# Expert weights as separate gate and up chunks, and all gate matmuls ahead of all up matmuls

## The reference, cut to what matters

```python
def expert_block(args):
    tok, e = args
    xb = xt_pad[tok]
    gate, up = jnp.split(xb @ w_gu[e] + b_gu[e], 2, axis=-1)
    gate = jnp.minimum(gate, SWIGLU_LIMIT)
    up = jnp.clip(up, -SWIGLU_LIMIT, SWIGLU_LIMIT)
    act = (up + 1) * (gate * jax.nn.sigmoid(SWIGLU_ALPHA * gate))
    return act @ w_dn[e] + b_dn[e]
```

## Time and profile before

| | |
|---|---|
| runs | 2408.28, 2408.59, 2414.71 us (median 2408.59) |
| profiled execution: its own time | 2408.47 us |
| profiled execution: span of the trace | 2406.7 us |
| mean granted TensorE clock | 0.963 |
| PE busy | 2178.1 us (91% of the span) |
| DVE, ACT, POOL busy | 747.0, 482.2, 65.4 us |
| moved by DMA | 591.29 MB in 158854 packets |

### The profile page before, as it was taken

One profiled execution on the slowest core, in us unless ns is written; L12 is line 12 of the kernel. 1 busy time (PEld: TensorE's weight loads), 2 busy tenths in 40 slices (PEclk: granted clock), 3 DMA queues, 4 the chain that ended last, 5 costly groups with the idle time before them and its releaser, 6 DMA issues.

```text
span 2406.7 us, 29048 instructions
## 1 busy us (share of the span) xinstructions
PE 2178.1 (91%) x11393; PEld 1161.2 (48%) x11394; DVE 747.0 (31%) x1825; ACT 482.2 (20%) x934; POOL 65.4 (3%) x79
## 2 busy tenths in 40 slices
PE   5999996899999998999889986997989997999998
PEld 4744453333333333333333334644454446888873
DVE  1696232122222221222211213242022254787100
ACT  1011111111111111111111101032021105887100
POOL 0000000000000000000000001000000000212000
PEclk8999997999999999999999998999999997999999
DMA  9554664769999998999966996443233141132241
GB/s 346 201 175 165 225 231 189 326 265 418 418 418 417 418 418 331 418 418 418 418 245 273 418 394 244 144 154 126 105 118 140 70 154 65 71 106 71 82 173 43
DMA packets 158854, 591.29 MB, mean 246 GB/s; under 512 B 5323, under 2 KB 6927, under 8 KB 125887
## 3 DMA queue, kind: packets, MB, share of 16 engines
q1 hardware_dynamic: 152512, 573.08, 60.8%
q0 software_dynamic: 4384, 16.40, 1.9%
q10 hardware_dynamic: 1887, 0.81, 0.1%
HBM read 589.23 MB, written 1.05 MB: 245 GB/s over the span
## 4 chain that ended last, share of the span: by engine, by line
PE 81%; DMA 6%; ACT 4%; DVE 4%; issue 2%; DVEq 1%; ACTq 0%; SPq 0%
PE PS L591 24%; PE PS L861 17%; PE PS L579 10%; PE PS L883 9%; PE PS L1049 4%; DMA W<-in_w_gu 3%; PE PS L895 2%; DMA W<-in_w_dn 2%; PE PS L854 1%; PE PS L1119 1%; PE PS L818 1%; PE PS L648 1%; DVE BIG L1833 1%; PE PS L831 1%; DVE BIG L1829 1%
## 5 line engine op out<-in xcount | busy, mean ns | idle before, releaser
L591 PE MATMUL PS<-W,BIG 128*128 128x512 f32 x1344 | 586.3, 598 | 5.0 <-DVE BIG L2245 2.9
L861 PE MATMUL PS<-W,BIG 128*64 128x512 f32 x2048 | 451.1, 598 | 3.2 <-DMA W<-in_w_gu 3.2
L591 PEld LDWEIGHTS PS<-W,BIG 128*128 128x128 f32 x1344 | 256.9, 192 | 325.1 <-issue 318.3
L861 PEld LDWEIGHTS PS<-W,BIG 128*64 128x64 f32 x2048 | 148.5, 138 | 305.3 <-issue 293.7
L579 PE MATMUL PS<-BIG,W 128*128 128x256 f32 x1088 | 240.8, 384 | 2.1 <-ACT BIG L348 2.1
L883 PE MATMUL PS<-W,BIG 128*64 128x512 f32 x1024 | 226.8, 595 | 8.4 <-ACT BIG L1317 8.4
L579 PEld LDWEIGHTS PS<-BIG,W 128*128 128x128 f32 x1088 | 209.5, 193 | 33.2 <-ACT BIG L348 3.3
L1827 DVE TENSOR_SCALAR BIG<-PS 128x512 f32<-128x512 f32 (+1 forms) x38 | 24.7, 650 | 426.7 <-PE PS L861 380.4
L883 PEld LDWEIGHTS PS<-W,BIG 128*64 128x64 f32 x1024 | 70.6, 137 | 144.0 <-issue 126.8
L1313 ACT ACTIVATE BIG<-BIG 128x512 f32<-128x512 f32 x32 | 20.2, 630 | 492.3 <-DVE BIG L1827 492.3
L1049 PE MATMUL PS<-BIG,W 128*128 128x256 f32 x448 | 105.3, 389 | 0.0
(11 more groups left out here) (453 smaller groups left out, 1917.8 us busy)
## 6 DMA issues: line engine op xcount, KB each, us to landing
W<-in_w_gu SPq DMA_DIRECT2D x128, 2048.0 KB, 14.1
W<-in_w_dn SPq DMA_DIRECT2D x64, 2048.0 KB, 15.6
W<-in_w_in SPq DMA_DIRECT2D x24, 2048.0 KB, 8.9
W<-in_w_mod SPq DMA_DIRECT2D x12, 2048.0 KB, 9.7
W<-in_gla_w_in SPq DMA_DIRECT2D x10, 2048.0 KB, 7.8
W<-in_s_w_in SPq DMA_DIRECT2D x8, 2048.0 KB, 8.9
W<-in_s_w_glu SPq DMA_DIRECT2D x8, 2048.0 KB, 8.0
W<-in_w_out SPq DMA_DIRECT2D x6, 2048.0 KB, 8.0
```

The lines of the kernel that those rows point to most:

```text
L591: ins = pe.matmul(ps[:, t, :], lhs(i * KT + k)[:, t * P:(t + 1) * P], w[:, k, :], start=i + k == 0, stop=last_chunk and k == KT - 1)
L861: ins = pe.matmul(PS[hh[h], g, :], XET[:, k, :], gu_w(k)[:, g * D + h * CH:g * D + (h + 1) * CH], start=False, stop=k == KT - 1, skip_grou ...
```

## The change

The w_gu chunks are cut another way. Before, chunk j held the whole rows of two k slices (two pieces of 8 KB for each partition). Now chunks 0 and 1 hold the gate columns of k 0 to 3 and 4 to 7, and chunks 2 and 3 the up columns, so that each partition gets four pieces of 4 KB. The matmul loops are turned: g is outermost, in the main part and in the extra block. gate_done is counted half way through the 32 matmuls instead of after the 30th. chunk_done for chunk 1 is counted one matmul later, at the first up matmul, since the last gate matmul already counts gate_done; the other counts stay at the same place.

```diff
@@ SP @@
                             if j < 4:
-                                sp.dma_start(flat_w.rearrange("p (a n) -> p a n", a=2), gu[:, 2 * j:2 * j + 2, :]) \
+                                sp.dma_start(flat_w.rearrange("p (a n) -> p a n", a=4),
+                                             gu[:, 4 * (j % 2):4 * (j % 2) + 4, (j // 2) * D:(j // 2 + 1) * D]) \
                                     .then_inc(w_landed[j], 16)
@@
-        def gu_w(k):
-            return W[:, k // 2].rearrange("p k n -> p (k n)").rearrange("p (a n) -> p a n", a=2)[:, k % 2, :]
+        def gu_w(k, g):
+            return W[:, 2 * g + k // 4].rearrange("p k n -> p (k n)").rearrange("p (a n) -> p a n", a=4)[:, k % 4, :]
@@ extra_block @@
-                for k in range(KT):
-                    if k % 2 == 0:
-                        landed(e, k // 2)
-                    for g in range(2):
+                for g in range(2):
+                    for k in range(KT):
+                        if k % 4 == 0:
+                            landed(e, 2 * g + k // 4)
                         for q in range(4):
-                            ins = pe.matmul(PS[qq[q], g, 0:T], XETX[:, k, :], gu_w(k)[:, g * D + q * T:g * D + (q + 1) * T],
+                            ins = pe.matmul(PS[qq[q], g, 0:T], XETX[:, k, :], gu_w(k, g)[:, q * T:(q + 1) * T],
                                             start=False, stop=k == KT - 1, skip_group_check=True)
@@ expert @@
-                for k in range(KT):
-                    if k % 2 == 0:
-                        landed(e, k // 2)
-                    for g in range(2):
+                for g in range(2):
+                    for k in range(KT):
+                        if k % 4 == 0:
+                            landed(e, 2 * g + k // 4)
                         for h in range(2):
-                            ins = pe.matmul(PS[hh[h], g, :], XET[:, k, :], gu_w(k)[:, g * D + h * CH:g * D + (h + 1) * CH],
+                            ins = pe.matmul(PS[hh[h], g, :], XET[:, k, :], gu_w(k, g)[:, h * CH:(h + 1) * CH],
                                             start=False, stop=k == KT - 1, skip_group_check=True)
-                        if k == KT - 1 and g == 0:
+                            if k == 0 and g == 1 and h == 0:
+                                ins.then_inc(chunk_done, 1)
+                        if k == 3:
+                            ins.then_inc(chunk_done, 1)
+                        elif k == KT - 1 and g == 0:
                             ins.then_inc(ev("gate_done"), 1)
-                    if k % 2 == 1 and k < KT - 1:
-                        ins.then_inc(chunk_done, 1)
                 ins.then_inc(ev("up_done"), 1)
```

## The result

The changed kernel takes 2418.41 us in the median of 20 runs (2416.57 to 2427.64); the kernel before took 2409.46 in 20 runs (2405.66 to 2416.94). The ratio is 1.0038, with a 95% interval of 1.003 to 1.0047. The forecast was 2420.3, inside a range of 2413 to 2428. By the medians the change costs 9.0 us; by the two profiled executions, which are rather low for the kernel before and rather high for the one after, 11.25 us (2408.47 and 2419.72).

The account below looks back on a forecast made before the run. The DMA queue was taken to set the pace for 23 expert loads, PE to bound the rest. Longer w_gu chunks cost 12.4 us, the early gate gains 0.6, sum 11.8: 2408.5 + 11.8 = 2420.3 us, range 2413 to 2428.

Parts of the forecast that it names:

- What bounds the kernel: Experts' stage: the DMA queue sets the pace in series of 14 and 9 loads, so 23 loads lie on the path.
- The cut of the w_gu chunks: w_gu loads in the two series: 4 KB pieces make each of 92 chunks 0.135 us longer, 12.4 us (11.5 to 13.3).
- the first stall: PE's first wait for weights in a series: forecast at its 8th expert, expert 10, and expert 24 in the second.
- the 14.1 that I reckoned: Time the queue has in hand before PE stalls: 11 x 1.36 - 0.86 = 14.1 us.
- Half rows cost what whole rows do: w_gu pieces of half a row priced like w_dn's 4 KB pieces, 410 GB/s; rival of dear half rows, 2449 us, chance 0.06.
- The line of 8 ns and 37 ns per KB: Queue time per piece, drawn through the 8 and 4 KB rates; gives 84 ns for 2 KB, where w_in_2 has 84.7.
- Piece length is free: Rival for the weight loads: one rate whatever the piece, only extra blocks count, 2407.9 us, no change; chance 0.10.
- Early gate: Activation: gain 0 in an ordinary expert, 0.15 us in each of four extra blocks, 0.6 us in all.
- Turned loops: Main part: the same 32 matmuls with the same tiles in another order, no cost.
- chunk_done of chunk 1 one matmul later: Load issue: two passes, some 0.4 us later, hidden; without cover it would be 0.4 us once per series.
- the cover of 1.5 us: Start of a series: the second load is asked for 1.5 us before the queue is free, which hides the later count.
- The clock falls in the new stalls: Rival for PE after waits of 1.9 us: five at 1.4 us would add 7 us, 2427 us; chance 0.04.

Follow-up runs that it names:

- the queue relieved: Kernel before and changed kernel, each with the second w_dn chunk cut to 32 bytes per partition, for timing only: 2390.88 us and 2384.48 us.
- the paired rows: Kernel before with its loops, each partition holding pairs of neighbouring weight rows (w_gu 16 KB, w_dn 8 KB pieces): 2401.45 us, ratio 0.997.
- the filler: 12 more matmuls in each extra block's gap; on the turned extra block 2408.47 us, on the late-count kernel 2426.18, with paired rows and turned extra block 2396.85.
- the late gate: Changed kernel with gate_done counted near the end of the up matmuls again, in main part and extra block: 2423.61 us, ratio 1.0057.

## Why the prediction was right

**What bounds the kernel.** Right: 23 expert loads on the path, as two unbroken transfers. It is what made a change of packet sizes worth anything; with the queue relieved the same change gained 6.4 us.

**The cut of the w_gu chunks, 92 x 0.135 = 12.4 us.** Right in mechanism, too small in size. The period gives (30.72 - 30.10) / 4 = 0.155 us a chunk, 14.3 in all, and the two series together 15.5. The chunk now takes 5.12 us, the upper end of what I had for w_dn; I took the middle. Of the 1.2 us between 14.3 and 15.5 the slow second 5 us of each series hold 1.1. It goes with the first stall, which came one expert sooner than forecast: at 30.72 - 28.74 = 1.98 lost per expert, seven experts use up 13.9, and PE waited 0.75 in the seventh, so the series had 13.9 - 0.75 = 13.1 in hand and not the 14.1 that I reckoned.

**Half rows cost what whole rows do.** Right: 409 GB/s in w_gu and 410 in w_dn. Pieces of 2 KB of the same matrix came to 387, of 16 KB and 8 KB together to 426. The line of 8 ns and 37 ns per KB (of 1000 bytes) held from 2 to 16 KB: it gives 427 and 421 GB/s for the two pieces of the paired rows, and 426 was measured over both. The 17 us that I expected of them, where 7.5 came, rested on a slip in working it out, and it left out the late loads ahead of expert 0 and the half clock in extra blocks.

**Piece length is free** (rival): refuted. The Trainium skill, "DMA: Bandwidth & Descriptors", section "Specifications", has 512 B as enough for the full rate; in these runs 2, 4 and 8 KB differ by 9%. The estimate of 0.23 us per expert load, by the Trainium skill, the same page, section "Why small descriptors are slow (HBM only)", compares with a measured 0.62.

**Early gate.** Right where it was priced: 0 in an ordinary expert (the wait is 0.44 before and after), 0.15 us in an extra block (1.52 to 1.37). What it may do through the clock was not in the prediction. Over all ten profiles without the filler, 10 of 26 blocks that no weight load holds up ran partly at half clock with an early gate, and 10 of 18 with a late one. That doesn't tell them apart, and whether part of the 5 us of the late gate comes from there stays open.

**Turned loops: 0.** Right as far as it shows: ordinary experts kept 28.74, and turning the extra block alone cost nothing.

**chunk_done of chunk 1 one matmul later: hidden.** Probably wrong, by 0.55 us a series. The second load is asked for 0.83 us later and not 0.4, and the cover of 1.5 us left out that a load moves nothing in the first microsecond behind its issue (0 GB/s from 498.88 to 499.88). All seven profiles with this count have 4.26 or 4.27 us to the second load of the first series and 337 to 373 GB/s in the second 5 us; the six without it have 3.43 or 3.42 and 424 to 439. The shorter pieces came with it each time, so it was not tested by itself.

**The clock falls in the new stalls** (rival): no. After each stall of 1.47 us the next 16 passes took 3.65, full speed. In the extra block of expert 25 it did fall: behind a wait of 3.20 us, where the kernel before waited 1.38, 32 passes took 3.58 instead of 1.93. The queue's last landing comes later than that (1220.74), so nothing came of it. By luck one half clock even went away: the last down half of expert 16 took 1.93 instead of 3.30, which is the -1.35 in the table.

**What was missing.** The loads of a ring do not only serve their own stage. The first w_gu loads run ahead of the experts beside a small load that the path waits for, and shorter pieces gave 1 to 2 us back there, and some of the clock behind it. The forecast came out close (11.8 against 11.25 by the profiles, 9.0 by the medians) because this and the clock's luck offset a queue term that was 3.1 us too small (15.5 against 12.4). That closeness is luck; the mechanism is not.

## What to carry to other kernels

Where a stage runs its DMA queue without a pause, the length of a contiguous piece is a price on the path, even between 4 and 8 KB; where a turned loop would cut rows, price that first, and give each partition whole or neighbouring rows if you can. Price it from the kernel's own saturated stretches by piece length, and count only the loads between the first issue with an empty queue and the landing that PE waits for. A later request for the second load counts too when the queue starts empty. Where the queue has slack, the same cut is free or better, so the answer of one stage is not that of another.

## What the runs showed of the hardware

- The rate of a saturated queue of 2 MB loads by piece: 387 GB/s at 2 KB (also with loads of 1 MB), 410 at 4 KB, 421 at 8 KB, 426 with 16 KB for w_gu and 8 KB for w_dn.
- A load of 512 KB from POOL's queue lands later the longer the pieces of the stream beside it: it was waited for until 9.9 to 10.6 us behind its issue at 8 KB and 11.6 at 16 KB, and had landed after 8.4 to 8.8 us at 4 KB.
- Gaps of 1.4 to 1.5 us in the extra blocks leave TensorE's clock at 2.4 GHz in one execution and drop it to 1.2 in the next, 1.7 us each time. After a wait of 3.19 us the same code took 1.93 us for 32 passes (922.42), after 3.05 it took 3.33, and after 3.20, later in the same execution as the first, 3.58 (1210.55). Matmuls in the gap kept it up in all of 12 blocks.
- Four transposes of the activation that read every second column took 0.75 us instead of 0.66.
- With 24 passes more in the extra block's code, the bias matmuls of the ordinary experts, which do not run it, took 0.25 us longer (1.27 against 1.02).
